# Norms between the stages of a two-block network: both token halves together, or one half behind the other

## What is computed

```python
f = swiglu(rmsnorm(h, ffn1_pre_g[i]), ...); h = h + 0.5 * rmsnorm(f, ffn1_post_g[i])
m = mixer(rmsnorm(h, mix_pre_g[i]), ...);   h = h + rmsnorm(m, mix_post_g[i])
f = swiglu(rmsnorm(h, ffn2_pre_g[i]), ...); h = h + 0.5 * rmsnorm(f, ffn2_post_g[i])
```

```python
x = layer_norm(DEEPNORM_ALPHA * x + mix, ln1_g[layer], ln1_b[layer])   # mix: conv or attention, and memory attention
x = layer_norm(DEEPNORM_ALPHA * x + ffn, ln2_g[layer], ln2_b[layer])   # ffn: dense, then 8 experts, top 2
```

## Time and profile before

| | us |
|---|---|
| median of 3 runs | 3175.75 |
| the runs | 3181.72, 3175.75, 3175.73 |
| the profiled execution, by its span (the page lists no other time for it) | 3176.3 |
| TensorE busy | 3005.6 (95%) |
| VectorE busy | 2219.6 (70%) |
| ScalarE busy | 1702.3 (54%) |
| mean granted TensorE clock, share of full speed | 0.974 |

### The profile page before, as it was taken

How to read it: one execution, slowest core, us unless ns; L and a number is a source line. 1 busy time by engine, 2 the same in 40 slices (tenths; PEclk the granted TensorE clock), 3 DMA queues, 4 the chain that set the end, 5 groups by cost and what they waited for, 6 DMA issues and landing times.

```text
span 3176.3 us, 52632 instructions
## 1 busy us (share of the span) xinstructions
PE 3005.6 (95%) x20975; PEld 2686.9 (85%) x20975; DVE 2219.6 (70%) x2599; ACT 1702.3 (54%) x1966; POOL 74.2 (2%) x68
## 2 busy tenths in 40 slices
PE   8998899999989988898999999999799999999997
PEld 7998898989989988888989897999577877787776
DVE  5778975755557779856555645556568888888887
ACT  4445566334444455664344444444456776667665
POOL 0000003000000000031000000000000000000000
PEclk9998999999999989999999999999899999999999
DMA  7553342446555533433455553555079999999995
GB/s 237 164 165 97 105 133 94 147 140 205 174 165 192 167 112 94 121 120 107 160 183 174 183 179 121 175 193 173 14 253 365 335 337 350 327 327 344 350 327 201
DMA packets 488737, 619.92 MB, mean 195 GB/s; under 512 B 34689, under 2 KB 439059, under 8 KB 488595
## 3 DMA queue, kind: packets, MB, share of 16 engines
q1 hardware_dynamic: 488595, 617.91, 59.2%
HBM read 616.81 MB, written 1.05 MB: 195 GB/s over the span
## 4 chain that ended last, share of the span: by engine, by line
PE 78%; DVE 13%; ACT 5%; issue 3%; DMA 0%; DVEq 0%; SPq 0%; ACTq 0%
PE PS L1076 13%; PE PS L617 12%; PE PS L618 12%; PE PS L619 12%; PE PS L670 12%; DVE w_lo L1633 3%; PE PS L1101 3%; PE PS L1103 3%; PE PS L1102 3%; ACT w_hi L1176 2%; PE PS L761 1%; PE PS L1053 1%; ACT w_hi L1565 1%; PE PS L1111 1%; PE PS L799 1%
## 5 line engine op out<-in xcount | busy, mean ns | idle before, releaser
L617 PE MATMUL PS<-x_hi,w_hi 128*128 128x256 f32 x3360 | 970.2, 289 | 15.7 <-DVE x_lo L2093 8.3
L618 PE MATMUL PS<-x_hi,w_lo 128*128 128x256 f32 x3360 | 960.8, 286 | 0.0
L619 PE MATMUL PS<-x_lo,w_hi 128*128 128x256 f32 x3360 | 960.1, 286 | 0.0
L1633 DVE TENSOR_TENSOR w_lo<-raw,w_hi 128x2048 fp32r<-128x2048 f32 x313 | 711.6, 2288 | 334.2 <-ACT w_hi L1176 333.6
L1176 ACT ACTIVATE w_hi<-raw 128x2048 fp32r<-128x2048 f32 x313 | 598.7, 1913 | 395.6 <-PE PS L670 246.6
L617 PEld LDWEIGHTS PS<-x_hi,w_hi 128*128 128x128 f32 x3360 | 655.6, 195 | 26.3 <-issue 13.3
L618 PEld LDWEIGHTS PS<-x_hi,w_lo 128*128 128x128 f32 x3360 | 655.6, 195 | 2.0
L619 PEld LDWEIGHTS PS<-x_lo,w_hi 128*128 128x128 f32 x3360 | 655.1, 195 | 0.0
L1076 PE MATMUL PS<-w_hi,x_hi 128*128 128x512 f32 x704 | 284.8, 405 | 3.1 <-DVE stage L2287 2.3
L1076 PE MATMUL PS<-w_lo,x_hi 128*128 128x512 f32 x704 | 276.3, 392 | 0.0
L1076 PE MATMUL PS<-w_hi,x_lo 128*128 128x512 f32 x704 | 275.0, 391 | 0.0
(11 more groups left out here) (404 smaller groups left out, 4631.8 us busy)
## 6 DMA issues: line engine op xcount, KB each, us to landing
XC<-in_w_gu_moe_dram SPq DMA_DIRECT2D x176, 512.0 KB, 9.2
raw<-in_w_gu_moe_dram SPq DMA_DIRECT2D x132, 512.0 KB, 8.2
raw<-in_w_in_dram SPq DMA_DIRECT2D x64, 1024.0 KB, 5.7
raw<-in_ffn_w_gate_dram SPq DMA_DIRECT2D x44, 1024.0 KB, 5.4
raw<-in_ffn_w_up_dram SPq DMA_DIRECT2D x44, 1024.0 KB, 6.5
raw<-in_ffn_w_down_dram SPq DMA_DIRECT2D x44, 1024.0 KB, 5.0
raw<-in_w_down_moe_dram SPq DMA_DIRECT2D x32, 1024.0 KB, 10.3
G<-in_w_down_moe_dram SPq DMA_DIRECT2D x32, 1024.0 KB, 9.6
```

The costliest lines, as they stand in the source:

```text
L617: mm(dst, w_hi[:, slot, w0:w0 + P], hi, start=start, stop=False, skip_group_check=True)
L618: mm(dst, w_lo[:, slot, w0:w0 + P], hi, start=False, stop=False, skip_group_check=True)
L619: return mm(dst, w_hi[:, slot, w0:w0 + P], lo, start=False, stop=True, skip_group_check=True)
L1633: tt(w_lo[:, slot, :], raw[:, slot, :], w_hi[:, slot, :].bitcast(F32), SUB)\
```

## The change

- `token_chunk` signals `half_summed` after kt 1, half 0: six products before the chunk's end. It does so in every token chunk, and the counters step over the chunks that nobody waits for.
- `post_norm`, both engines: half 0 (ScalarE's square and its own root, VectorE's gain, reciprocal, update of H) is done first, from `half_summed` on; then half 1, after the chunk's end. VectorE starts a half once ScalarE has squared it (`squared`); the signal `weighed` goes. A root and a reciprocal for each half.
- `pre_norm`: the same, a root, reciprocal and scaling for each half. The copy of `prm` goes ahead of the squares.
- `layer_norm`: VectorE starts half 0 at `half_summed`; gain, reciprocal and shift run half by half, with a wait for itself after each gain. The last layer norm has no early signal but the new order.
- `warm` in the seven waits: 10 products, not 16.

```diff
@@ TensorE
                             for b in range(2):
                                 last = mm(PS[:, bank + 2 * t + b, :], left, right[...],
                                           start=False, stop=True, skip_group_check=True)
+                        if kt == 1 and t == 0:
+                            last.then_inc(s["half_summed"], n.one("half_summed"))
                 last.then_inc(s["chunk_used"], n.one("chunk_used"))
...
-                warm(4, 16)
+                warm(4, 10)
                 turn_stream(scaled, "scaled_ready")
                 mixer()
-                warm(0, 16)
+                warm(0, 10)
...
@@ ScalarE
-            def root(bias, scale):
-                act.wait_ge(s["act_step"], n.last("act_step"))
-                fn(sums[:, 1, :], sums[:, 0, :], ACT.Sqrt, bias=eps[:, bias:bias + 1], scale=scale)\
+            def root(src, t, small, scale, spare=unused, event="act_step", **how):
+                fn(spare[:, t, :], src[:, t, :], ACT.Square, accum_out=sums[:, 0, t:t + 1], **how)\
+                    .then_inc(s[event], n.one(event))
+                act.wait_ge(s[event], n.last(event))
+                fn(sums[:, 1, t:t + 1], sums[:, 0, t:t + 1], ACT.Sqrt, bias=eps[:, small:small + 1], scale=scale)\
                     .then_inc(s["rooted"], n.one("rooted"))
...
             def pre_norm(g0, slots):
 
-                for t in range(2):
-                    act.wait_ge(s["h_ready"], n.due("h_ready"))
-                    square_sum(H, t, "act_step")
                 if g0 == 0:
                     act.wait_ge(s["prm_psum"], n.due("prm_psum"))
                     fn(prm[:, :], PS[:, 7, 0:192], ACT.Copy).then_inc(s["prm_ready"], n.one("prm_ready"))
                     act.wait_ge(s["prm_ready"], n.last("prm_ready"))
-                root(0, 1.0 / D)
+                for t in range(2):
+                    act.wait_ge(s["h_ready"], n.due("h_ready"))
+                    root(H, t, 0, 1.0 / D)
...
-            def post_norm(half, acc=BY_TOKEN):
+            def post_norm(half, acc=BY_TOKEN, chunks=STEPS):
 
                 near_root()
-                wait_used(pos[0] + 1)
-                square_sum(acc, 0, "squared")
-                act.wait_ge(s["weighed"], n.due("weighed"))
-                square_sum(acc, 1, "act_step")
-                root(3 if half else 0, (4.0 if half else 1.0) / D)
+                for t in range(2):
+                    if t == 0:
+                        act.wait_ge(s["half_summed"], n.due("half_summed", chunks))
+                    else:
+                        wait_used(pos[0] + 1)
+                    root(acc, t, 3 if half else 0, (4.0 if half else 1.0) / D, event="squared")
...
@@ VectorE
-            def inverse_root():
+            def inverse_root(t):
                 dve.wait_ge(s["rooted"], n.due("rooted"))
-                then(v.reciprocal(sums[:, 1, :], sums[:, 1, :]))
+                then(v.reciprocal(sums[:, 1, t:t + 1], sums[:, 1, t:t + 1]))
...
-                inverse_root()
                 for t in range(2):
+                    inverse_root(t)
                     ts(scaled[:, t, :], H[:, t, :], sums[:, 1, t:t + 1], None, MULT)\
...
                 dve.wait_ge(s["gain_in"], n.due("gain_in", 16))
-                wait_used(pos[0] + 1)
-                tt(weighted[:, 1, :], acc[:, 1, :], gain, MULT).then_inc(s["weighed"], n.one("weighed"))
-                dve.wait_ge(s["squared"], n.due("squared"))
-                tt(weighted[:, 0, :], acc[:, 0, :], gain, MULT)
-                inverse_root()
+                n.due("half_summed", chunks)
                 for t in range(2):
+                    dve.wait_ge(s["squared"], n.due("squared"))
+                    then(tt(weighted[:, t, :], acc[:, t, :], gain, MULT))
+                    inverse_root(t)
                     stt(H[:, t, :], weighted[:, t, :], sums[:, 1, t:t + 1], H[:, t, :], MULT, ADD)\
                         .then_inc(s["h_ready"], n.one("h_ready"))
...
-            def layer_norm(src, split=True, late=None):
+            def layer_norm(src, chunks=0, split=True, late=None):
 
                 for t in range(2):
+                    if chunks and t == 0:
+                        dve.wait_ge(s["half_summed"], n.due("half_summed", chunks))
+                    if chunks and t == 1:
+                        wait_used(pos[0] + 1)
                     then(stt(H[:, t, :], H[:, t, :], ALPHA, src[:, t, :], MULT, ADD, accum_out=sums[:, 0, t:t + 1]))
                     then_on(ts(sums[:, 2, t:t + 1], sums[:, 0, t:t + 1], -1.0 / D, None, MULT), "centered")
                 dve.wait_ge(s["gain_in"], n.due("gain_in", 32))
                 for t in range(2):
-                    ins = stt(weighted_2[:, t, :], H[:, t, :], sums[:, 2, t:t + 1], gain, ADD, MULT)
-                then(ins)
-                inverse_root()
-                for t in range(2):
+                    then(stt(weighted_2[:, t, :], H[:, t, :], sums[:, 2, t:t + 1], gain, ADD, MULT))
+                    inverse_root(t)
                     stt(H[:, t, :], weighted_2[:, t, :], sums[:, 1, t:t + 1], shift, MULT, ADD)\
                         .then_inc(s["h_ready"], n.one("h_ready"))
```

More of the change, by code:

```diff
@@ L131 @@
     "step": {
-        "weights_ready": 3, "staged": 2, "chunk_used": 3, "gate_a": 1, "up_a": 1, "raw_a": 16, "raw_b": 16,
+        "weights_ready": 3, "staged": 2, "chunk_used": 3, "half_summed": 1, "gate_a": 1, "up_a": 1, "raw_a": 16, "raw_b": 16,
         "raw_c": 16, "hi_ready": 3, "silu_done": 2, "dve_step": 2},
@@ L148 @@
     "layer": {
-        "weights_ready": 123, "gains_in": 160, "prm_ready": 1, "scaled_ready": 6, "x_ready": 14, "staged": 76,
+        "weights_ready": 123, "half_summed": 26, "gains_in": 160, "prm_ready": 1, "scaled_ready": 6, "x_ready": 14, "staged": 76,
         "s5_ready": 1, "s5c_ready": 1, "c_ready": 8, "b_ready": 8, "c_evicted": 41, "cv_ready": 8, "in_ready":
@@ L359, in build @@
         names = ("raw_a raw_b raw_c hi_ready weights_ready chunk_used consts_in x_in params_in params_done "
-                 "gains_in prm_psum prm_ready setup_done h_ready squared rooted xh_ready x_ready gain_in weighed scaled_ready turned logit_ready "
+                 "gains_in prm_psum prm_ready setup_done h_ready half_summed squared rooted xh_ready x_ready gain_in scaled_ready turned logit_ready "
                  "gate_a up_a silu_done staged c_evicted tap_done silu_conv c_ready c_psum b_ready in_psum in_ready cv_ready "
@@ L1184, in near_root @@
                 fn(eps[:, 4:5], eps[:, 0:1], ACT.Sqrt)
-            def root(bias, scale):
-                act.wait_ge(s["act_step"], n.last("act_step"))
-                fn(sums[:, 1, :], sums[:, 0, :], ACT.Sqrt, bias=eps[:, bias:bias + 1], scale=scale)\
+            def root(src, t, small, scale, spare=unused, event="act_step", **how):
[3 more added lines that the diff above has]
+                fn(sums[:, 1, t:t + 1], sums[:, 0, t:t + 1], ACT.Sqrt, bias=eps[:, small:small + 1], scale=scale)\
                     .then_inc(s["rooted"], n.one("rooted"))
-            def square_sum(src, t, event, spare=unused, **how):
-                last = fn(spare[:, t, :], src[:, t, :], ACT.Square, accum_out=sums[:, 0, t:t + 1], **how)
-                last.then_inc(s[event], n.one(event))
             def pre_norm(g0, slots):
-                for t in range(2):
-                    act.wait_ge(s["h_ready"], n.due("h_ready"))
-                    square_sum(H, t, "act_step")
                 if g0 == 0:
@@ L1449, in _ @@
                 mixer()
-                post_norm(False, OUT_BY_TOKEN)
+                post_norm(False, OUT_BY_TOKEN, 4)
                 pre_norm(32, ((C_OUT + 3) % RING,))
@@ L1466, in layer_norm @@
                     act.wait_ge(s["centered"], n.due("centered"))
-                    square_sum(H, t, "act_step", unused_2, bias=sums[:, 2, t:t + 1])
-                root(2, 1.0 / D)
+                    root(H, t, 2, 1.0 / D, unused_2, bias=sums[:, 2, t:t + 1])
                 if split:
@@ L1668, in pre_norm, with post_norm @@
                     convert(slot)
-            def post_norm(acc=BY_TOKEN):
+            def post_norm(acc=BY_TOKEN, chunks=STEPS):
                 dve.wait_ge(s["gain_in"], n.due("gain_in", 16))
-                wait_used(pos[0] + 1)
-                tt(weighted[:, 1, :], acc[:, 1, :], gain, MULT).then_inc(s["weighed"], n.one("weighed"))
-                dve.wait_ge(s["squared"], n.due("squared"))
-                tt(weighted[:, 0, :], acc[:, 0, :], gain, MULT)
-                inverse_root()
+                n.due("half_summed", chunks)
                 for t in range(2):
+                    dve.wait_ge(s["squared"], n.due("squared"))
+                    then(tt(weighted[:, t, :], acc[:, t, :], gain, MULT))
+                    inverse_root(t)
                     stt(H[:, t, :], weighted[:, t, :], sums[:, 1, t:t + 1], H[:, t, :], MULT, ADD)\
@@ L2079, in _ @@
                 mixer()
```

(11 more changed lines are left out.)

## The result

The changed kernel takes 3177.92 us (median of 20 runs, 3175.75 to 3185.61), the kernel before, run beside it, 3174.71 us (20 runs, 3169.45 to 3182.50). The ratio is 1.0015, 95% interval 1.0008 to 1.0022: 0.15% slower, within the 0.2% that the forecast took for no change, though the interval's upper end lies just above it. The medians lie 3.2 us apart, where 3.3 was forecast; the ratio is some 4.8 us. The profiled execution took 3185.61 us, the longest of the twenty, of which its span is 3183.7.

The account below looks back on a forecast made before the run. TensorE was taken as the bound, with time to win where it waits at norms. 6.4 us won against 8.4 + 1.3 lost to the clock gave 3.3 more than the profiled 3176.3; forecast 3179.0 us, range 3168 to 3187.

Parts of the forecast that it names:

- The win of 6.4 us: Whole kernel: gains at the waits and layer norms, less losses at the start and norms, sum to 6.4 us less.
- the loss of 8.4 + 1.3 us: TensorE's clock: falls in four of seven waits cost 8.4 us; the first products after 907 at lower clock, 1.3.
- The four waits: Waits at 211, 708, 1112 and 1613 us: early signal and order by halves win 1.2 us each, 4.7 in all.
- At 907: Wait without constants: half 0's transposes run before half 1 is scaled, 1.8 us won; lower clock behind it costs 1.3.
- Block 2: Wait at 1813 us: VectorE converts until the end, then has the same four passes; nothing won, 0.
- The layer norm behind the first attention: Early signal lets VectorE start 1.2 us earlier; less the second reciprocal and drain, 0.85 us won.
- The one behind the second: Layer norm behind the second attention: VectorE starts earlier by the early signal, 0.88 us won.
- Dense FFN: Layer norm behind it: no earlier start, while a second reciprocal and a drain lose 0.33 us.
- The start: First norm: squares queue behind the copy of prm, with two roots; 1.15 us lost (0.7 to 2.6).
- The clock: TensorE's granted clock falls in four of the seven waits, at 2.1 us each: 8.4 us more (0 to 18).
- the second rival: Clock falls in all seven waits, router's small products 1 to 3 us slower: 3186.9 us; chance 0.24.
- The first: Rival: clock holds in all waits, 3170.6 us (3168 to 3172); chance 0.28.

Follow-up runs that it names:

- Number 1: The changed kernel with 16 constant products, not 10, in all seven waits: 3170.06 us, ratio 0.9983 to the kernel before.
- 10: The changed kernel with 13 constant products, not 10, in each of the seven waits: 3170.16 us, ratio 0.9989 to the kernel before.
- number 5: The changed kernel with 16 constant products but no early signal, both halves waiting for the chunk's end: 3174.52 us, ratio 0.9997 to the kernel before.
- number 2: The kernel before with 10 constant products, not 16, in the seven waits and nothing else changed: 3188.85 us, ratio 1.0041.
- number 11: Another single execution of the changed kernel, unaltered, to look at the stretch through the first attention: 3177.72 us.
- 9: The changed kernel run again, unaltered, beside the kernel before: 3177.61 us, ratio 1.0014.
- number 3: The changed kernel with the copy of prm behind the squares again in the very first norm: 3175.63 us, ratio 0.9999 to the kernel before.

## Why the prediction was right

**The class and the sum held, and so did their two halves.** The win of 6.4 us and the loss of 8.4 + 1.3 us could have cancelled by accident, and single terms did miss by up to half a microsecond either way, as the paragraphs below show. Number 1 takes the 8.4 away but keeps the 1.3 at 907, so by the forecast it should win 5.1: 0.17% is 5.4 us (1.6 to 8.9). The changed kernel beside numbers 1 and 10 shows the loss by itself: 7.9 us, and 7.45 on the same chip.

**The four waits: 1.18 us each forecast, 1.1 measured** where the clock holds (11.38 to 10.28), 0.9 where it falls. x_hi comes 8.3 us behind the last product at the second wait (forecast 8.2). The early signal was the condition, as number 5 shows, and VectorE's last `w_lo` ended in time for it.

**At 907** it is 1.8 us less from first product to first product of the two stages (199.2, before 201.0), as forecast. The lower clock over the first products behind it came too, and cost more than the 1.3 forecast: from the stage's first product to the constants behind it, it is 193.9 us, before 192.1, so 1.8 us. In numbers 2 and 5, where the clock was back ahead of that product, it is 192.1 as before. What the order won at 907 the clock took back in full.

**Block 2**: 6.47 us from the memory's transposes to the first product, before 1819.57 - 1813.09 = 6.48; forecast 0. **The layer norm behind the first attention**: 9.37 us from constants to first product, before 10.30, so 0.93 won (forecast 0.85), with the clock fallen. **The one behind the second**: 9.05 us from constants to the router's small products, before 9.48, so 0.43 won (forecast 0.88). **Dense FFN**: half 1's transposes start 8.81 us behind the constants' start, before 8.43: 0.38 lost (forecast 0.33). **The last norm** takes 8.42 us on VectorE, before 8.10: 0.32 (forecast 0.33).

**The start: 1.15 us lost was forecast, 0.6 to 0.8 measured** (first x_hi 15.17, before 14.35; first product 18.03, before 17.45). The forecast let the squares queue behind the copy where it had stood, at 10.21; in this execution the copy ran at 9.86, 0.35 us sooner, since the transposes of the parameters, which wait for a load, came at 9.24 and not at 9.60. Square, root, square, root then took 2.75 us (10.22 to 12.97), about as forecast. So the smaller loss is the luck of a load. One pair of executions can't size it: number 2, whose start is that of the kernel before, has its first product at 16.59, number 11, whose start is the changed one, at 18.93.

**The clock: four of seven forecast, four of seven in the profiled execution**, at 2.1 us each forecast, 2.2 each in number 2. But the four was partly luck: in the two other profiled executions of the same kernel (9 and 11) it fell in three of the seven, and held in the first wait. What recurs in all three is the fall at the dense FFN's norm, at the router, and at 907. The forecast named no waits for its four; the layer norms are the weak ones. Over the five profiled executions that have 10 constants in the waits concerned, the clock fell at the dense FFN five times in five (idle pieces of 1.6 us on both sides of a burst), at the router five in five and behind the first attention three in five (0.2 us ahead of the first burst, 1.6 behind it), and in the waits ahead of a pre-norm's transposes in four of twenty. At the router the forecast had 1 to 3 us for the small products, in the second rival alone; they cost 3.1 us here. Part is bought back: from the constants to the first expert product it is 30.4 us, before 28.6, in number 1 27.6.

**The rivals.** The first (clock holds everywhere, 3170.6) is nearly what number 1 does: 3170.06, with an interval of some 7 us around it, so the closeness is chance, and with the clock held everywhere but at the dense FFN and the router. The second (all seven fall) comes nearly true in the old order, number 2, with six, and not in the new one: there the burst of half 0 stands in the idle time. The third is refuted by the 0.16 us at 211.50 and the 10.28 us of the wait.

**What the transposes count for.** At the second wait 5.8 us lie between the last constant and the first product, holding transposes alone, and the granted clock stayed at 1.00; in number 2, after 3.75 us with nothing in them it fell four times in four, ahead of the transposes or within 1.1 us of their start. So the bursts count as work here. The Trainium skill, TensorE: Matmul & The Clock Gate, Part 4: PE-mode transpose, has it that they do not; by that rule number 2 and the changed kernel would fall alike, and the trace disagrees. The argument's own row, the rise at 919.74 after cold transposes, repeats at 907 in numbers 2 and 5: transposes from 920.56 and 917.98, the clock back at 924.5 and 921.1, first products at 924.87 and 922.29. But in the changed kernel it does not: after as long a burst from 917.16 the clock rose only at 926, and likewise in numbers 1, 3, 9, 10 and 11. The transposes there start sooner after the fall (1.3 us in the changed kernel, 3.0 in the kernel before); whether that decides it was not tried.

What stays open: whether number 3 is faster, what brings the clock back late at 907 in the new order, and what in the first attention decides its draw. By the profiled executions the account is good to a few microseconds and not better, as that draw alone is 6.6.

## What to carry to other kernels

Constant products that fill a wait are part of its price: with them thinned from 16 to 10, a norm that had become 1.1 us shorter in each wait paid some 2 us for each fall of the clock, and with 13 or 16 it kept the win. When a wait is made shorter, size its filler by the idle piece ahead of the next real work (0.6 us held, 1.9 us fell in four of twenty, 3.75 us each time), look at the idle pieces behind it too (1.6 us on both sides of a burst fell each time), and do not go by how much of it seems idle capacity. Here the order by halves paid only through the early signal that starts the first half; look first whether the engine that would use it is free by then.

## What was not expected of the hardware

One program takes 115.8 or 122.4 us for the same stretch, depending on whether the clock falls within it: a difference larger than the whole change. A single profiled execution of this kernel can't be compared with another to better than that; the span of the changed kernel's stands 7.4 us above the one before, where the medians say 3.2.

Products of 8 columns feel the clock nearly in full: 32 of them take 3.74 us at 2.4 GHz and 6.84 us at 1.2 GHz.
